# HGRN2's level differences moved from VectorE to a GpSimd program with four level buffers

## What is computed

```python
q, f, i, g = jnp.split(hn @ w_in, 4, axis=-1)
q = jax.nn.silu(q)
fg = lower_bound + (1.0 - lower_bound) * jax.nn.sigmoid(f)
k, log_f = 1.0 - fg, jnp.log(fg)
# per head (8 heads of 128), per chunk:
bc = jnp.cumsum(lf_c, axis=2)
dec = jnp.exp(bc[t] - bc[s])           # for s <= t, per channel
scores = sum_d q[t, d] * k[s, d] * dec[t, s, d]
o = scores @ v + (q * jnp.exp(bc)) @ S
S = jnp.exp(bc[last]) * S + (k * jnp.exp(bc[last] - bc)).T @ v
o = o * lax.rsqrt(jnp.mean(o * o, -1) + eps) * norm_w * jax.nn.silu(g)
```

## Time and profile before

| what | value |
|---|---|
| median of three runs | 3319.44 us (3308.86 to 3335.03) |
| profiled execution: its time | 3339.86 us |
| profiled execution: span | 3338.1 us, 54485 instructions |
| TensorE matmul busy over the span | 2628.3 us, 79% |
| VectorE busy | 1984.0 us, 59% |
| ScalarE busy | 1572.1 us, 47% |
| GpSimd busy | 374.8 us, 11% |
| mean granted TensorE clock | 0.88 |

### The profile page before, as it was taken

The page is one execution under the profiler, slowest core; times in us unless marked ns, Lnnn a source line. Parts: engine busy times, 40 slices in busy tenths (PEclk is TensorE's granted clock), DMA queues, the critical chain, the costliest instruction groups (busy, mean ns, idle before and its releaser), DMA issues. The chain is left out here.

```text
span 3338.1 us, 54485 instructions
## 1 busy us (share of the span) xinstructions
PE 2628.3 (79%) x18232; PEld 2204.6 (66%) x18232; DVE 1984.0 (59%) x2201; ACT 1572.1 (47%) x1904; POOL 374.8 (11%) x342
## 2 busy tenths in 40 slices
PE   4997125888648699999991899999939679999992
PEld 3776004778336578888871788888827568888881
DVE  3331573444432589889875365666621478898894
ACT  3111442222211278888862354555420258888882
POOL 0000001000000022232221000000000013333320
PEclk8999567899868599999995899999869589999996
DMA  2111000000011499999964110111020479999984
GB/s 82 44 44 28 4 3 2 3 3 3 1 51 43 148 333 379 383 384 380 375 246 167 38 32 25 32 32 30 7 101 0 134 287 375 378 383 381 384 330 179
DMA packets 221098, 520.46 MB, mean 156 GB/s; under 512 B 43952, under 2 KB 99248, under 8 KB 220976
## 3 DMA queue, kind: packets, MB, share of 16 engines
q1 hardware_dynamic: 202544, 485.15, 39.5%
q0 software_dynamic: 18432, 33.60, 2.7%
HBM read 501.86 MB, written 50.33 MB: 165 GB/s over the span
## 5 line engine op out<-in xcount | busy, mean ns | idle before, releaser
L1493 DVE TENSOR_TENSOR w_low<-w_raw,w_high 128x1024 fp32r<-128x1024 f32 x768 | 894.9, 1221 | 32.7 <-DVEq L51 21.7
L1288 ACT CAST w_high<-w_raw 128x1024 fp32r<-128x1024 f32 x768 | 755.2, 1048 | 112.0 <-ACTq L51 112.0
L1387 PE MATMUL ps<-w_high,x_high 128*128 128x512 f32 x1024 | 415.1, 405 | 8.9 <-PEq L51 6.9
L1391 PE MATMUL ps<-w_high,x_low 128*128 128x512 f32 x1024 | 404.3, 395 | 0.0
L1390 PE MATMUL ps<-w_low,x_high 128*128 128x512 f32 x1024 | 402.5, 393 | 0.0
L1387 PEld LDWEIGHTS ps<-w_high,x_high 128*128 128x128 f32 x1024 | 195.7, 191 | 52.2 <-issue 15.7
L1711 PE MATMUL ps<-h_high,w_high 128*128 128x512 f32 x512 | 212.5, 415 | 18.4 <-PEq L51 18.4
L1391 PEld LDWEIGHTS ps<-w_high,x_low 128*128 128x128 f32 x1024 | 194.4, 190 | 42.8
L1390 PEld LDWEIGHTS ps<-w_low,x_high 128*128 128x128 f32 x1024 | 195.3, 191 | 37.4
L1387 PE MATMUL ps<-w_high,hidden_high 128*128 128x512 f32 x512 | 201.6, 394 | 6.8 <-PEq L51 6.8
L1711 PE MATMUL ps<-h_high,w_low 128*128 128x512 f32 x512 | 202.1, 395 | 0.0
(11 more groups left out here) (400 smaller groups left out, 5166.5 us busy)
## 6 DMA issues: line engine op xcount, KB each, us to landing
w_raw<-in_moe_w_gate SPq DMA_DIRECT2D x256, 512.0 KB, 5.7
w_raw<-in_moe_w_up SPq DMA_DIRECT2D x256, 512.0 KB, 5.9
w_raw<-in_moe_w_down SPq DMA_DIRECT2D x256, 512.0 KB, 5.8
w_raw<-expert_rows SPq DMA_DIRECT2D x32, 512.0 KB, 9.9
w_tiles<-in_c_w_in SPq DMA_DIRECT2D x32, 512.0 KB, 4.0
w_tiles<-in_ab_w_in SPq DMA_DIRECT2D x22, 512.0 KB, 3.9
h_rows<-hn_moe SPq DMA_DIRECT2D x16, 512.0 KB, 3.6
residual<-in_x SPq DMA_DIRECT2D x8, 512.0 KB, 6.7
```

Of the source, the lines that this page charges most:

```text
L1288: act.copy(wh[:, p, :], raw[:, p, :]).then_inc(high_made, 1)
L1387: ins = pe.matmul(ps[:, bank, :], high, w_h, start=first, stop=False)
L1391: return pe.matmul(ps[:, bank, :], low, w_h, start=False, stop=final)
L1493: dve.tensor_tensor(wl[:, p, :], raw[:, p, :], wh[:, p, :].bitcast(F32), ALU.subtract).then_inc(low_made, 1)
```

## The change

GpSimd gets a loop over the eight heads. In each it waits for `bc_pool` (given by VectorE behind the scan), makes the seven level differences in order and then the KD difference, all with `tensor_tensor`. Before each level difference it takes one `e_free`; four are given at the start and one at every `picked`. Before the KD difference it takes `kd_free`, given at the start and behind the variance. VectorE loses all differences; nothing else of its order changes, nor does that of ScalarE, TensorE or SyncE.

```diff
+                def diff(lv):
+                    take(pool, s["e_free"])
+                    v, hw = level_view(BC[:], lv), HLEVELS[lv]
+                    ref = v[:, :, hw - 1:hw].to_broadcast([P, S // (2 * hw), 2 * hw])
+                    pool.tensor_tensor(level_view(E[:, lv % 4, :], lv), v, ref, ALU.subtract).then_inc(s["diff_ready"], 1)
+
+                with pool.Fori(0, HEADS):
+                    take(pool, s["bc_pool"])
+                    for lv in range(NL):
+                        diff(lv)
+                    take(pool, s["kd_free"])
+                    bc = BC[:].rearrange("p (n q) -> p n q", q=P)
+                    pool.tensor_tensor(KD[:].rearrange("p (n q) -> p n q", q=P), bc[:, :, P - 1:P].to_broadcast([P, TT, P]), bc,
+                                       ALU.subtract).then_inc(s["diff_ready"], 1)
...
+                dve.sem_inc(s["e_free"], 4)
+                dve.sem_inc(s["kd_free"], 1)
...
                 def picked(lv, n=1):
                     take(dve, s["order"], n)
                     dve.sem_inc(gram_free[lv % 2], 1)
-
-                def diff(lv):
...
-                    dve.tensor_tensor(level_view(E[:, lv % 4, :], lv), v, ref, ALU.subtract).then_inc(s["diff_ready"], 1)
+                    dve.sem_inc(s["e_free"], 1)
...
                     dve.sem_inc(s["bc_ready"], 1)
-                    diff(0)
-                    diff(1)
+                    dve.sem_inc(s["bc_pool"], 1)
...
                     pick_diagonal()
-                    diff(2)
-                    diff(3)
                     for lv in range(2, NL):
                         pick(lv - 2)
                         scale(lv, par, behind=lv - 2)
                         if more and lv == 5:
                             low(2)
-                        if lv + 2 < NL:
-                            diff(lv + 2)
-                        if lv + 2 == NL:
-
-                            bc = BC[:].rearrange("p (n q) -> p n q", q=P)
-                            dve.tensor_tensor(KD[:].rearrange("p (n q) -> p n q", q=P), bc[:, :, P - 1:P].to_broadcast([P, TT, P]), bc,
-                                              ALU.subtract).then_inc(s["diff_ready"], 1)
...
                     dve.sem_inc(s["var_ready"], 1)
                     dve.sem_inc(s["tail_free"], 1)
+                    dve.sem_inc(s["kd_free"], 1)
```

More of the change, by code:

```diff
@@ L1632, in hgrn @@
                  "v_turned", "v_rows_ready", "kd_turned", "kd_rows_ready", "ds_done", "s_ready", "score_ready",
-                 "o_done", "sq_ready", "sq_summed", "var_ready", "rstd_ready", "tail_free", "o_read")
+                 "o_done", "sq_ready", "sq_summed", "var_ready", "rstd_ready", "tail_free", "o_read", "bc_pool", "e_free", "kd_free")
         s = {n: sem(n) for n in names}
@@ L1944, in picked @@
                     dve.sem_inc(gram_free[lv % 2], 1)
-                def diff(lv):
-                    v, hw = level_view(BC[:], lv), HLEVELS[lv]
-                    ref = v[:, :, hw - 1:hw].to_broadcast([P, S // (2 * hw), 2 * hw])
-                    dve.tensor_tensor(level_view(E[:, lv % 4, :], lv), v, ref, ALU.subtract).then_inc(s["diff_ready"], 1)
+                    dve.sem_inc(s["e_free"], 1)
                 def scale(lv, par, behind=None):
```

## The result

The changed kernel takes 3348.8 us (median of 15 runs; 3323.4 to 3360.3), the kernel before 3319.4 (15 runs). The ratio is 1.0064, 95% interval 1.0036 to 1.0092: 12 to 31 us slower. It is that of the two means, which differ by 21.2 us; the medians differ by 29.4. Two later kernels had one execution each far above the rest (4802 us in "Two back and held", 5401 us in "All on GpSimd, kept apart"), which their ratios leave out. The spans of the two profiled executions, 3358.5 and 3338.1 us, differ by 20.4. The heads account for 16.7 of it; 4.2 lie ahead of the first scan (1896.50 against 1892.35), in stages that the change does not touch.

What follows compares the result with a forecast made beforehand. TensorE was taken to bound the middle heads, with ScalarE's 1.75 us of slack at the border. Borders 12, clock 8, first head 3, last head -3 made +20 us on 3319.4: 3339 us, range 3307 to 3366.

Steps and rivals of the forecast that it cites:

- The border: Between heads: later exponentials of differences 0 and 1 delay `Ln` and `gram` by 1.7 us, 12 us over seven borders.
- the difference: Time of one level or KD difference on GpSimd, taken as 2.3 us between bounds of 1.85 and 2.9.
- the stop by `low(0)`: At the border, the weight subtraction directly behind the scan stops GpSimd's difference 0 for 1.1 us.
- The lower bound worked out from the selects: Least time of a GpSimd difference, from one-input selects with two inputs read one behind the other: 1.85 us.
- the estimate of 2.25 that stood beside the sum: GpSimd difference time of 2.25 us from the engine reference's 4497 ns on 2048 columns; said to change nothing in the sum.
- Short runs: Possible GpSimd cost of 10.7 ns a run: level 6 would pay 5.5 us more, hidden in a middle head.
- The clock: TensorE's clock dips behind the longer border wait at all seven borders, five more at 1.6 us: 8 us.
- The first head: Slower differences 0 and 1 ahead of `pick_diagonal`, and difference 1 stopped by level 0's scaling: +3 us.
- The last head: Differences 2 and 3 made ahead, so an earlier start at about the old pace per level: -3 us.
- Rival B: GpSimd's running differences hold VectorE's two-tile reads: 14 us more at borders, 8 in the last head; 3361 us, 1.5 in 10.

Runs made afterwards that it cites:

- Two back and held: Changed kernel with differences 0 and 1 returned to VectorE and GpSimd held ahead of difference 2 until VectorE comes to `pick_diagonal`; ratio to the kernel before 0.9989.
- All on GpSimd, kept apart: Changed kernel with `low(0)` behind the variance and GpSimd held ahead of difference 2 until VectorE comes to `pick_diagonal`; ratio to the kernel before 0.9983.
- the third experiment: Changed kernel with GpSimd held ahead of difference 2 until VectorE issues `scale(1)`, and `low(0)` moved behind the variance; ratio to the kernel before 1.0044.
- the three experiments with GpSimd idle: Kernel before with an extra ScalarE copy ahead of `Ln` (1.0030), with three projection portions behind the sum of squares (0.9963), or those plus `low(0)` behind the variance (0.9971).
- the shift: Kernel before with three portions of the next head's projection moved from ahead of the sum of squares to behind it; ratio 0.9963.
- the first experiment: Changed kernel with differences 0 and 1 back on VectorE ahead of `bc_pool`, GpSimd doing the rest without being held; ratio to the kernel before 1.0095.
- the delay on ScalarE: Kernel before, GpSimd idle, with one more ScalarE copy of 640 columns between the variance and `Ln` at each of seven borders; ratio 1.0030.

## Why the prediction was right

It said 3339 and slower by 20 us, within 1%; measured were 3349 and a ratio worth 21 us. All 20 were forecast inside the phase; there the two traces differ by 16.7, and 4.2 more lie in stages that the change does not touch. The mechanism was right: VectorE relieved for nothing in the middle heads, ScalarE's slack overrun at the border, the clock behind the longer wait. No level product in a middle head waits. The terms, however, were off in both directions.

- **The border**: 1.7 us a head predicted, 0.8 measured. The term mis-sized is the difference: 2.3 us taken, 1.9 measured when nothing lies beside it (3.81 for two in the third experiment; KD 1.89), 2.35 beside a scaling. Twice 0.4 us less is what `Ln` came earlier than forecast; the stop by `low(0)`, 1.1 us, was right (2.93 against 1.92). The lower bound worked out from the selects, 1.85, was nearly the value, and the estimate of 2.25 that stood beside the sum was too long as well. Nor do seven borders pay: at the seventh there is no `low(0)`, and its wait is as before.
- **Short runs** cost nothing: level 6, with 512 runs, takes 2.35 us like level 4 with 128, and like KD with 8 runs where that lies beside a scaling too (2.34, last head). The selects' cost per run does not carry over.
- **The clock**: 1.6 us a dip, right; four dips more than before and not five. In the middle heads together 11.1 us (six heads of 71.6 against a mean of 69.7) where border and clock were to give 20 over seven borders.
- **The first head**: +3 predicted, +5.3 measured. The step that failed is that VectorE is not held.
- **The last head**: -3 predicted, +0.3 measured. From norm product to last pick it is 1.5 us shorter (27.5 against 29.0): levels pass at 3.3 us each as before, and only the start is earlier. But the rest to the variance is 1.8 longer: the state products take 3.75 us in place of 2.02, at a granted clock of 0.50 against 1.00. Those 1.8 us are not shown to be the change's: the products take 3.5 to 3.8 us in all eleven other traces, the three experiments with GpSimd idle among them, and 2.02 in that of the kernel before alone. TensorE's timeline of the changed kernel, below it of the one before, and of the kernel before with the shift:

```profile
2436.95 3.75 PE L1780 MATMUL ps<-v_rows,k_rows 128*128 128x128 f32 x16 [1.28 <-PEq L51]
```

```profile
2417.91 2.02 PE L1765 MATMUL ps<-v_rows,k_rows 128*128 128x128 f32 x16 [1.28 <-PEq L51]
```

```profile
2406.26 3.75 PE L1765 MATMUL ps<-v_rows,k_rows 128*128 128x128 f32 x16 [1.28 <-PEq L51]
```

Rival B is therefore true as a mechanism and was wrong only in its price. I had weighed it by VectorE instructions of 8 columns beside mask selects, which showed no more than that such short ones are not held for a select's length. Scalings of up to 2.48 us in the changed kernel and a weight subtraction of 3.05 in the first experiment are held by a running difference; and a difference beside a scaling takes 0.46 us more. The rule of the SBUF — State Buffer page of the Trainium skill (Who interferes with whom), that the first to issue keeps the shared ports and the other waits, is stated there of VectorE's two-port modes; of instructions with two SBUF inputs the page says that they contend with GpSimd's reads. The trace agrees with it for these too, in both directions: 2.93 us for a difference that `low(0)` preceded, and 2.28 for a scaling that a difference preceded. In the middle heads the holding hid behind `Ln`, so B's 14 us at the borders were not paid, and in the last head the levels kept their 3.3 us in place of B's 4.4; its cost was the first head's 3.4 us, which no term of B had. That the sum came out near is in part luck: terms too large and a term missing made up for each other, and where 20 us were put on borders and clock, 11 were measured.

What stays open: why TensorE's clock dips behind some waits of 1.90 us and not behind others, and why the state products ran at the full clock in one trace alone.

## What to carry to other kernels

Before moving work off an engine, find the chain that sets the period and see whether that engine is on it; then look at who stands next behind the moved step in a fixed order, since here a ScalarE instruction with 1.75 us of slack was the one that paid. What GpSimd and VectorE take from each other when both read SBUF costs time only where the held step has no slack: the same differences cost 2.4 us a middle head when they overlapped the border, and nothing when they were kept out of it and overlapped scalings inside the head. An idle stretch of the feeding engine ahead of the critical step is better spent by moving cover behind it, which took 9.6 us off the phase (ratio 0.9963, 0.9930 to 0.9995) with two changed numbers.

## What was not expected of the hardware

- A GpSimd subtraction on 128x1024 with one input broadcast takes 1.9 us with nothing beside it, 1.6 times VectorE's 1.22, and 2.35 beside a scaling, with 8 runs as with 512.
- GpSimd can start between two VectorE instructions that are queued back to back, and then hold the second: two of 1.22 us became 4.15 us.
- Predicated copies with the mask in SBUF and the data in PSUM are not held (0.71 to 0.75 us inside running differences).
- Waits of one length did not all end in the same clock: behind 2.75 us of waiting (the delay on ScalarE) five middle borders dipped and one did not, behind 2.70 us all six of the changed kernel did; behind 1.90 us it was two of six before, four of six with `low(0)` late, three of six with all kept apart; behind 0.96 us none.
